# Block attention with a third score buffer: scores formed three tiles ahead instead of two, and their PSUM bank released by VectorE's read

## What is computed

```python
    s = q @ k.T * scale + bias_of_distance      # block attention, causal
    o = softmax(s) @ v
    y_b = o @ w_attn_out
    s = qm @ mk.T * (MEM_DH ** -0.5)            # memory attention
    y_c = (softmax(s) @ mv) @ w_mem_out
    merged = sigmoid(ga + bg[0]) * y_a + sigmoid(gb + bg[1]) * y_b + sigmoid(gc + bg[2]) * y_c
```

## Time and profile before

| | us |
|---|---|
| median of 3 runs | 1746.24 (1745.93 to 1752.27) |
| profiled execution, device time | 1747.59 |
| its span, first to last instruction | 1745.8 |
| block attention, tiles 0 to 31 (888.7 to 1031.6 us of the span) | 142.9 |
| memory attention, tiles 32 to 47 (1108.8 to 1194.1 us) | 85.3 |

### The profile page before, as it was taken

The page is one execution under the profiler, slowest core; times in us unless marked ns, Lnnn a source line. Parts: engine busy times, 40 slices in busy tenths (PEclk is TensorE's granted clock), DMA queues, the critical chain, the costliest instruction groups (busy, mean ns, idle before and its releaser), DMA issues.

```text
span 1745.8 us, 19842 instructions
## 1 busy us (share of the span) xinstructions
PE 1598.2 (92%) x7636; PEld 1261.4 (72%) x7636; DVE 609.9 (35%) x939; ACT 670.8 (38%) x996; POOL 725.5 (42%) x616
## 2 busy tenths in 40 slices
PE   7899648699999999899988898999998999999995
PEld 4699535478888888678865567787776888887874
DVE  3664372433333200324024331242305455554002
ACT  2532441354444322332233444453323555554231
POOL 0465101344444544444421136344534455555452
PEclk8999877899999999999998999999999999999998
DMA  8553202412222223212411123222321222222321
GB/s 354 190 222 144 73 1 48 113 48 96 96 96 96 84 85 94 100 39 83 145 48 37 37 78 116 73 73 84 108 74 49 69 85 90 94 96 84 97 85 48
DMA packets 27145, 162.78 MB, mean 93 GB/s; under 512 B 3240, under 2 KB 3368, under 8 KB 12360
## 3 DMA queue, kind: packets, MB, share of 16 engines
q1 hardware_dynamic: 23616, 151.01, 25.2%
q10 hardware_dynamic: 3464, 10.88, 2.4%
HBM read 157.15 MB, written 4.72 MB: 93 GB/s over the span
## 4 chain that ended last, share of the span: by engine, by line
PE 67%; DVE 9%; issue 9%; POOL 8%; ACT 3%; DMA 3%; POOLq 0%; SPq 0%; DVEq 0%; ACTq 0%
PE ps L1445 58%; POOL WL L664 6%; PE ps L1426 2%; DMA adaw<-w_ada_dram 2%; PE ps L1648 1%; DMA raw<-w_up_dram 1%; PE ps L1662 1%; DVE dl L1131 1%; PE ps L1675 1%; DVE nt L1107 1%; DVE xT L1137 1%; PE ps L1433 1%; DVE S L1367 1%; ACT S L829 1%; POOL WL L630 1%
## 5 line engine op out<-in xcount | busy, mean ns | idle before, releaser
L630 POOL TENSOR_TENSOR WL<-raw,WH 128x512 fp32r<-128x512 f32 (+2 forms) x368 | 399.1, 1113 | 671.7 <-ACT WH L739 671.6
L1445 PE MATMUL ps<-hH,WH 128*128 128x512 f32 x1136 | 458.1, 403 | 10.8 <-DVE hL L1123 5.6
L1445 PE MATMUL ps<-hL,WH 128*128 128x512 f32 x1136 | 451.3, 397 | 0.0
L1445 PE MATMUL ps<-hH,WL 128*128 128x512 f32 x1136 | 451.2, 397 | 0.0
L664 POOL TENSOR_TENSOR WL<-raw,WH 128x512 fp32r<-128x512 f32 x176 | 247.2, 1435 | 247.8 <-ACT WH L861 247.8
L1445 PEld LDWEIGHTS ps<-hH,WH 128*128 128x128 f32 x1136 | 215.0, 189 | 68.7 <-issue 14.7
L739 ACT ACTIVATE WH<-raw 128x1024 fp32r<-128x1024 f32 (+3 forms) x184 | 160.2, 896 | 248.5 <-PE ps L1445 232.0
L1445 PEld LDWEIGHTS ps<-hH,WL 128*128 128x128 f32 x1136 | 214.9, 189 | 52.2
L1445 PEld LDWEIGHTS ps<-hL,WH 128*128 128x128 f32 x1136 | 214.8, 189 | 49.9 <-issue 0.5
L1445 PE MATMUL ps<-hidH,WH 128*128 128x512 f32 x352 | 139.6, 397 | 1.1 <-POOL WL L664 1.1
L1445 PE MATMUL ps<-hidH,WL 128*128 128x512 f32 x352 | 137.1, 390 | 0.0
(11 more groups left out here) (230 smaller groups left out, 2269.0 us busy)
## 6 DMA issues: line engine op xcount, KB each, us to landing
raw<-w_up_dram SPq DMA_DIRECT2D x44, 1024.0 KB, 4.9
raw<-w_in_dram SPq DMA_DIRECT2D x36, 1024.0 KB, 4.9
adaw<-w_ada_dram SPq DMA_DIRECT2D x20, 1024.0 KB, 7.1
raw<-w_down_dram SPq DMA_DIRECT2D x16, 768.0 KB, 4.1
raw<-w_down_dram SPq DMA_DIRECT2D x16, 640.0 KB, 3.9
adap<-w_ada_dram SPq DMA_DIRECT2D x4, 1024.0 KB, 18.3
xT<-x_dram ACTq DMA_DIRECT2D x2, 2048.0 KB, 11.2
raw<-w_mem_kv_dram SPq DMA_DIRECT2D x4, 1024.0 KB, 4.8
```

The source lines that it names most:

```text
L630: pool.tensor_tensor(WL[:, d % 2, ks, cols], raw[:, d % 2, ks, cols], WH[:, d % 2, ks, cols].bitcast(F32), ALU.subtract).then_inc(lo_done, 1)
L1445: mm = pe.matmul(out, lhs[x], rhs[y], start=(first and i == 0), stop=(last and i == 2))
```

## The change

A third score buffer `S2c` is laid out beside the two in `S2`, and tile n uses number n % 3 in all places. `attend()` puts the scores of three tiles ahead of the first mid2, and front2(n+3) where front2(n+2) stood. DVE's bias step waits for T(n-3) instead of T(n-2). The score banks in PSUM stay two; S(n) now waits for DVE's bias step of tile n-2 (`s2_read`) where that tile is of the block attention, and still for its exponential where it is of the memory attention. The list keeps its number of steps and pieces, 128 with 38 and 64 with 48.

```diff
+        S2c = at("S2c", [P, S], 18)
...
-            tiles = [("front2", first), ("front2", first + 1)]
+            tiles = [("front2", first), ("front2", first + 1), ("front2", first + 2)]
             for n in range(first, last):
                 tiles += [("mid2", n)]
                 if n > first:
                     tiles += [("lo2", n - 1)]
-                if n + 2 < last:
-                    tiles += [("front2", n + 2)]
+                if n + 3 < last:
+                    tiles += [("front2", n + 3)]
                 tiles += [("back2", n)]
...
+        def scores2(n):
+            return (S2[:, 0, :], S2[:, 1, :], S2c[:])[n % 3]
...
-                if n >= 2:
-                    ve.wait_ge(pt2_done, n - 1)
+                if n >= 3:
+                    ve.wait_ge(pt2_done, n - 2)
...
             def front2(n):
                 kind, i, h, nb, c, row = tile2(n)
                 if n >= 2:
-
-                    pe.wait_ge(exp2_done, n - 1)
+                    pe.wait_ge(s2_read if TILES23[n - 2][0] == "self" else exp2_done, n - 1)
```

More of the change, by code:

```diff
@@ L950, in front2 @@
                 if kind == "self":
-                    t, scale = S2[:, n % 2, 0:P * nb], 1.0
+                    t, scale = scores2(n)[:, 0:P * nb], 1.0
                     src = t
                 else:
-                    t, scale = S2[:, n % 2, 0:P * nb], P ** -0.5
+                    t, scale = scores2(n)[:, 0:P * nb], P ** -0.5
                     src = ps[:, 4 + n % 2, 0:P * nb]
@@ L1353, in front2 @@
                     bias = (W0 if h < 4 else W1)[:, h % 4, S - w:S]
-                    ve.scalar_tensor_tensor(out=S2[:, n % 2, 0:w], in0=ps[:, 4 + n % 2, 0:w], scalar=DH ** -0.5, in1=bias,
+                    ve.scalar_tensor_tensor(out=scores2(n)[:, 0:w], in0=ps[:, 4 + n % 2, 0:w], scalar=DH ** -0.5, in1=bias,
                                             op0=ALU.mult, op1=ALU.add).then_inc(s2_read, 1)
                     ve.wait_ge(s2_read, n + 1)
-                    ve.tensor_reduce(md2[:, 0, n:n + 1], S2[:, n % 2, 0:w], X, ALU.max, negate=True).then_inc(negm2_ready, 1)
+                    ve.tensor_reduce(md2[:, 0, n:n + 1], scores2(n)[:, 0:w], X, ALU.max, negate=True).then_inc(negm2_ready, 1)
                 else:
@@ L1366, in mid2 @@
                 link(ve.reciprocal(md2[:, 2, n:n + 1], md2[:, 1, n:n + 1]))
-                ve.tensor_scalar(S2[:, n % 2, 0:w], S2[:, n % 2, 0:w], md2[:, 2, n:n + 1], None, ALU.mult
+                ve.tensor_scalar(scores2(n)[:, 0:w], scores2(n)[:, 0:w], md2[:, 2, n:n + 1], None, ALU.mult
                                  ).then_inc(p2_scaled, 1)
@@ L1661, in mid2 @@
                 for b in range(nb):
-                    mm = pe.transpose(ps[:, 6, P * b:P * b + P], S2[:, n % 2, P * b:P * b + P], ident)
+                    mm = pe.transpose(ps[:, 6, P * b:P * b + P], scores2(n)[:, P * b:P * b + P], ident)
                 mm.then_inc(pt2_done, 1)
```

## The result

| | before | changed |
|---|---|---|
| median of 8 runs each, side by side, us | 1749.27 (1745.93 to 1752.27) | 1755.20 (1751.29 to 1757.11) |
| ratio, 95% interval | | 1.0037 (1.0024 to 1.0051) |
| span of the profiled execution, us | 1745.8 | 1753.7 |
| block attention, us | 142.9 | 137.8 |
| memory attention, us | 85.3 | 95.9 |

The change costs 0.37%, some 6.5 us (the medians differ by 5.9). The forecast was 7.1 us, 1753.5. It was added to a median before of 1746.24; side by side the kernel before measured 1749.27, 3.0 us more, so the difference is the fair comparison and not the absolute time.

What follows compares the result with a forecast made beforehand. PE, busy 92% of the span, was taken as the bound, its block attention waits coming from DVE's order. Block attention -0.4 and memory attention +7.5 us gave +7.1, so 1753.5 us, range 1747 to 1761.

Steps and rivals of the forecast that it cites:

- Three ahead, bank, buffer: Both attentions: one more tile of lead, the earlier bank release and the third buffer give no direct gain, 0 us.
- The holes: Memory attention: merge work now before the scalings of tiles 36, 40, 44 costs 2.5 us each, 7.5 us together.
- Thirteen T without a cover: Block attention: transposes with no piece between the newest S and them wait for the scaling, 12.9 us in all.
- the two waits of V: Block attention: V(29) waits about 0.75 us for ACT's copy; a sigmoid with table loads closer to V(8) costs 0.4 us.
- the sign that it would fall to about 1 us: Block attention: the changed trace should show T(11) waiting about 1 us instead of 1.79.
- The slow scalings: Block attention: scalings before T 7, 17 and 27 fall into POOL's work and cost 1.5 us together.
- the dearer estimate: Block attention: by the shared port rule each slow scaling loses about 1.3 us, 2 us above the sum in all.
- The term 1.2 for T(16): Block attention: one uncovered transpose's share of the 12.9 us, with 0.25 added because S is one width further on.
- the start: Block attention: the third S fits the hole before T(0) and leaves the place behind it, gaining 0.2 us.
- both rivals on the clock: Clock falls in memory attention holes, +2 to +8 us, chance 0.25; block attention's half-clock stretch goes, 4.5 us, chance 0.14.
- my sum: Whole kernel: block attention -0.4 and memory attention +7.5 give +7.1 us, 1751 to 1756 us, chance 0.47.
- the clock's case: Memory attention: one to three clock falls in the new holes, 1755 to 1762 us, put at 1758, chance 0.25.

Runs made afterwards that it cites:

- f1: Changed kernel with VectorE's own list altered to scale tile n+1 before the newest tile's bias and maximum: 1727.05 us, 0.9886 of the kernel before.
- f2: Kernel before (two ahead, two buffers) with VectorE's list altered to scale tile n+1 before the bias of tile n+2: 1724.71 us, ratio 0.9869.
- e1: Changed kernel with its pieces put one step later again in both attentions, as in the kernel before: 1746.16 us, 0.9993 of the kernel before.
- e4: Kernel before with only the score bank's wait changed, to VectorE's bias step of the tile two back: 1747.04 us, ratio 1.0000.
- e2: Changed kernel with the pieces put back one step only in the memory attention: 1746.20 us, 0.9989 of the kernel before.
- g1: Changed kernel with both sums into merged of the memory attention's branch cut to one column each: 1749.94 us, 1.0007 of the kernel before.
- g2: The changed kernel run and traced once more, unaltered: 1755.19 us, 1.0035 of the kernel before.
- e3: Kernel before, two ahead and two buffers, with only its pieces one step earlier in both attentions: 1754.60 us, ratio 1.0036.

## Why the prediction was right, point by point

**The bound and the waits.** The reading of the earlier trace rows, that DVE's order and not the exponential makes T late, is shown by f1 and f2: mend the order and the waits go, with two tiles ahead as with three.

**Three ahead, bank, buffer: nothing.** Shown by e1 and e4, each to about 0.1%.

**The holes.** Forecast 4.94 us from S to T, a hole of 2.5 (2.14 to 2.67) before T(36), T(40) and T(44). Measured 4.90, and 2.47, 2.45, 2.45. Three holes are 7.4 us of the 7.5 forecast. The mechanism was right, and that 2.5 came so close is in part luck. I took less than the 2.67 of the sum because POOL might disturb the merge work less, and it took 3.13 us with one sum at 1.17 us, about as slow as before. What made up for it was the cover: PE's last matmul before T(36) ended 2.43 us after S started, where I had taken 2.27 from the start of S to the start of T.

**The block attention.** Thirteen T without a cover were named, T(11) among them, and just these waited, with T(0) and T(21). Their sum with the two waits of V is 16.2 + 0.8 + 0.7 = 17.7 us, forecast 17.3. Single terms were off and cancelled, which is luck: T(11) waited 1.75 us where I had 1.15, as long as the 1.79 before, so the sign that it would fall to about 1 us did not come true. The rest L1381 of tile 9 and a copy of 0.85 instead of 0.43 us beside POOL kept DVE in the merge work until 933.7, after the S of 932.08 that was to cover it. V(8) waited 0.8, not 0.4, and for DVE's `bufBL`, not for ACT's copy. The slow scalings cost 0.9 us, not 1.5: that of tile 7 took 0.87 us instead of 0.29, that of tile 17 0.74 instead of 0.42, and that of tile 27 was not slowed, so none lost the 1.3 us of the dearer estimate. The term 1.2 for T(16) was a slip, as 0.85 + 0.25 is 1.10; it waited 1.18. The first T came 3.36 us after the first S, against 3.37 before, so the start only hid the third S.

**The clock.** In the profiled execution both rivals on the clock happened and nearly cancelled, which is luck for the number, as my sum has neither: the stretch at half clock in the block attention was spared (PE's busy time -4.7 us) and two falls came behind the holes (+3.3 us; windows of 4 us at 0.61 and 0.57). The two windows: length, PE busy, granted clock, DMA share, GB/s:

```profile
1132.00:1136.00 4.00, 2.70 (x8) 0.61 0.37 126
...
1160.00:1164.00 4.00, 4.00 (x12) 0.57 0.00 0
```

The second trace had no fall in the memory attention, and 0.99 in the block attention. I priced a first fall at about 2 us, and the two came to 3.3. That the time of single executions ranges over 6 us around the median fits this, though which part of that range the clock makes was not measured. That the new order spared the stretch is not shown: four traces have the very same list in the block attention (the changed kernel, e2, g1, g2), and their clock there is 0.96, 0.94, 0.94 and 0.99, their length 137.8, 139.7, 139.7 and 134.9 us. The eleven traces of all kernels go from 0.93 to 0.99. The median of 1755.2 us lies in the interval of my sum (1751 to 1756) and at the lower end of the clock's case (1755 to 1762), so the time alone does not tell the two apart.

**The rule on small idle times.** I weighed the Trainium skill (TensorE: Matmul & The Clock Gate, the section on the second failure mode) on frequent small idle times, as a reason for a swing of the clock in all three places. Two traces with holes of 2.5 us (the changed kernel and e3) show two falls each, a third (g2) none, and g1 with holes of 1.4 us none. It is a risk per hole, not a rule for each.

## What to carry to other kernels

Working further ahead pays only if the late instruction is waiting for what the lead brings nearer; look first at what stands in front of it in its own engine's list. Here the same VectorE instructions in another order gave 22.8 us, and a third buffer nothing that could be measured. Where pieces are spread over a list by position, moving one step to its head moves every piece against the tiles, though the length of the list stays: print the order around the longest side job (here 3.1 us of merge work) and check that nobody waits for what stands right behind it.

## What the runs showed of the hardware that I had not expected

The granted clock differs between executions of the same program with the same waits: 0.96 with two falls in one trace of the changed kernel's memory attention, 1.00 in another, with the holes equal to 0.02 us. In the block attention the same two traces have 0.96 and 0.99 with the same waits. PE's busy time so differs by 3.0 us in the block attention (117.8 and 114.8) and by 2.9 us in the memory attention (86.4 and 83.6) without any cause in the program.
